# Two copies instead of one for the high part of the weights in the up projection groups without down tiles

## The reference, cut to what matters

```python
def block(xt):
    q = (xt @ wq).reshape(tb, PEER_HEADS, 2, PEER_HALF_DIM)
    ...
    gate = jax.nn.softmax(sc.astype(jnp.float32), axis=-1)
    pre = jnp.einsum("td,thkd->thk", xt, down[idx])
    act = (jax.nn.gelu(pre.astype(jnp.float32), approximate=False) * gate).astype(xt.dtype)
    return jnp.einsum("thk,thkd->td", act, up[idx])
```

## Time and profile before

| | |
|---|---|
| median of 3 runs | 2964.32 us (2959.3 to 2971.26) |
| profiled execution, its own time | 2967.73 us |
| its span | 2965.8 us |
| granted TensorE clock, mean over the span | 0.975 |
| busy: PE, PEld, DVE, ACT, POOL | 2742.1, 2529.3, 1888.9, 1127.9, 1075.9 us |

### The profile page before, as it was taken

One profiled execution on the slowest core, in us unless ns is written; L12 is line 12 of the kernel. 1 busy time (PEld: TensorE's weight loads), 2 busy tenths in 40 slices (PEclk: granted clock), 3 DMA queues, 4 the chain that ended last, 5 costly groups with the idle time before them and its releaser, 6 DMA issues.

```text
span 2965.8 us, 55557 instructions
## 1 busy us (share of the span) xinstructions
PE 2742.1 (92%) x20766; PEld 2529.3 (85%) x20766; DVE 1888.9 (64%) x3331; ACT 1127.9 (38%) x1682; POOL 1075.9 (36%) x444
## 2 busy tenths in 40 slices
PE   7899999989987999999988999999999889999997
PEld 5687777889987999999866877778999779999997
DVE  1663562299798554689817526533995975457887
ACT  1312320344487444333303124104445864443332
POOL 0000110478843656433300001004887245663332
PEclk9999999999999999999999999999999999999998
DMA  5222223255544566455452322233555446664543
GB/s 191 101 80 82 103 75 140 88 174 175 170 146 171 199 207 205 155 194 184 143 184 72 104 72 90 88 128 129 170 170 169 152 174 206 198 199 165 195 172 107
DMA packets 145453, 439.50 MB, mean 148 GB/s; under 512 B 62066, under 2 KB 63602, under 8 KB 126772
## 3 DMA queue, kind: packets, MB, share of 16 engines
q1 hardware_dynamic: 132548, 400.84, 39.7%
q10 hardware_dynamic: 12784, 37.00, 3.3%
HBM read 407.10 MB, written 30.15 MB: 147 GB/s over the span
## 4 chain that ended last, share of the span: by engine, by line
PE 61%; DVE 15%; issue 12%; POOL 8%; ACT 2%; DVEq 1%; DMA 0%; POOLq 0%; ACTq 0%; SPq 0%
PE banks L462 60%; POOL DHL L1903 7%; DVE arena L1356 3%; DVE OHE L1356 2%; DVE OHG L1356 2%; DVE ACTS L1356 1%; DVE AHL L1356 1%; ACT arena L983 1%; DVE UHL L1356 1%; POOL arena L1891 1%; DVE hT L1364 1%; DVE arena L1685 0%; DVE arena L1457 0%; DVEq L1356 0%; ACT L983 0%
## 5 line engine op out<-in xcount | busy, mean ns | idle before, releaser
L462 PE MATMUL banks<-HHL,DHL 128*128 128x264 f32 x6816 | 859.4, 287 | 23.6 <-POOL DHL L1903 12.1
L462 PEld LDWEIGHTS banks<-HHL,DHL 128*128 128x128 f32 x6816 | 844.2, 190 | 32.3 <-POOL DHL L1903 16.5
L462 PE MATMUL banks<-AHL,UHL 128*128 128x264 f32 x6144 | 773.3, 286 | 31.6 <-DVE AHL L1356 29.1
L462 PEld LDWEIGHTS banks<-AHL,UHL 128*128 128x128 f32 x6144 | 758.6, 189 | 41.9 <-issue 41.8
L1903 POOL TENSOR_TENSOR DHL<-ring,DHL 128x1024 fp32r<-128x1024 f32 x256 | 657.3, 2572 | 277.8 <-ACT DHL L983 276.0
L1356 DVE TENSOR_TENSOR xT<-xT,banks 128x264 f32<-128x264 f32 x1040 | 402.7, 423 | 388.8 <-PE banks L462 387.9
L462 PE MATMUL banks<-hT,ring 128*128 128x272 f32 (+1 forms) x2048 | 501.8, 403 | 9.7 <-issue 7.9
L1909 POOL TENSOR_TENSOR UHL<-ring,UHL 128x1024 fp32r<-128x1024 f32 x128 | 308.7, 2412 | 538.2 <-ACT UHL L983 538.2
L462 PEld LDWEIGHTS banks<-hT,ring 128*128 128x128 f32 x2048 | 394.4, 196 | 101.7 <-issue 23.1
L983 ACT ACTIVATE UHL<-ring 128x2048 fp32r<-128x2048 f32 x128 | 245.5, 1918 | 509.8 <-PE banks L462 486.7
L983 ACT ACTIVATE arena<-banks 128x264 f32<-128x264 f32 (+6 forms) x226 | 98.7, 455 | 635.9 <-PE banks L462 587.2
(11 more groups left out here) (118 smaller groups left out, 1925.1 us busy)
## 6 DMA issues: line engine op xcount, KB each, us to landing
ring<-down SPq DMA_DIRECT2D x256, 512.0 KB, 3.7
ring<-up SPq DMA_DIRECT2D x128, 1024.0 KB, 4.9
ring<-wm SPq DMA_DIRECT2D x100, 1024.0 KB, 5.0
hT<-second_gates SPq DMA_DIRECT2D x32, 528.0 KB, 4.9
second_gates<-ring ACTq DMA_DIRECT2D x12, 768.0 KB, 3.3
second_gates<-hT ACTq DMA_DIRECT2D x10, 768.0 KB, 3.3
ACTS<-extra_acts SPq DMA_DIRECT2D x2, 2112.0 KB, 9.8
arena<-hs ACTq DMA_DIRECT2D x2, 1280.0 KB, 6.1
```

The costliest lines, as they stand in the source:

```text
L462: return pe.matmul(out, lhsT, rhs, start=start, stop=stop)
```

## The change

In groups from MIXED on, ScalarE's one copy over both tiles becomes two copies of one tile each: tile 1, the one that GpSimd reads, first, and with it the release of GpSimd; then tile 0, which releases nobody. The AHL copy follows as before, with VectorE's release. In groups below MIXED the one copy stays.

```diff
-                    f(UHL[:, b, 0].rearrange("p a m -> p (a m)"),
-                      ring[:, RAWU + 2 * b:RAWU + 2 * b + 2].rearrange("p s k m -> p (s k m)"), ACT.Copy)\
-                        .then_inc(S["uhi_done"], 1)
+                    if g < MIXED:
+                        f(UHL[:, b, 0].rearrange("p a m -> p (a m)"),
+                          ring[:, RAWU + 2 * b:RAWU + 2 * b + 2].rearrange("p s k m -> p (s k m)"), ACT.Copy)\
+                            .then_inc(S["uhi_done"], 1)
+                    else:
+                        f(UHL[:, b, 0, 1], ring[:, RAWU + 2 * b + 1].rearrange("p k m -> p (k m)"), ACT.Copy)\
+                            .then_inc(S["uhi_done"], 1)
+                        f(UHL[:, b, 0, 0], ring[:, RAWU + 2 * b].rearrange("p k m -> p (k m)"), ACT.Copy)
                     f(AHL[:, b, 0], ACTS[:, bass.ds(turn * GRP + half_g * GRP, GRP), :], ACT.Copy)\
                         .then_inc(S["ahi_done"], 1)
```

## The result

The changed kernel is faster: 2941.35 us median (2935.73 to 2943.41, 6 runs) against 2965.52 us (2959.30 to 2971.26, 6 runs) for the kernel before. The ratio is 0.9903, with a 95% interval of 0.9889 to 0.9918. The profiled execution took 2936.94 us with a span of 2935.0, 30.8 us less span than before.

The account below looks back on a forecast made before the run. TensorE, busy 92% of the span, was taken as the bound, held back 33.2 us in groups 24 to 63; less 5.4 us remaining, the gain is 28 us, from 2964.3 to 2936 us, range 2928 to 2944, top set at 2950.

Parts of the forecast that it names:

- The bound and who is late: Groups 24 to 63: TensorE, pace 5.86 us a group, is held back 33.2 us by GpSimd's late start slowing VectorE.
- x = 0.87: Splitting ScalarE's UHL copy lets GpSimd start and end 0.87 us earlier, judged from ScalarE's DHL copies in the trace.
- What VectorE gets: VectorE's UHL low instruction, with GpSimd's cover shrunk to 0.33 us, takes 1.41 us.
- The margin of 0.13 us: In groups starting on time, the next could begin after 5.73 us, 0.13 before TensorE is ready at 5.86.
- the 0.14: VectorE's UHL low takes 1.22 us plus the time covered by GpSimd minus 0.14, a line through three covered cases.
- A pair gives back x up to 0.735: Two successive groups lose 0.735 us together; GpSimd starting x earlier wins back x, at most that 0.735.
- What is late next: Remainder over TensorE's pace: 0.63 us in group 25 plus 2.1 from late starts, 5.4 us in both layers, between 1.3 and 9.
- The late starts: ScalarE starts late three times in layer 0 on late loads, 0.7 us each; layer 1 taken alike.
- Rival 3: The late AHL copy holds up VectorE's low part and makes the kernel slower, 3000 us in its worst case; chance 0.03.
- a slip beyond the room: A later AHL copy, slip y, costs nothing up to about 0.75 us, then all of it; gain used up at 1.44.
- its last case: Both half copies take as long as the whole one, y = 1.9: 0.46 us per interval, 36 us over 78, 3000 us.
- TensorE's clock: A gapless TensorE might run slower; granted clock 1.00 (2.4 GHz) in the busy stretch ahead, so nothing was taken for it.

Follow-up runs that it names:

- a short GpSimd instruction: Kernel before, one copy kept, GpSimd making only 128 of its 1024 low-part columns in groups 24 to 63: 2935.07 us, 0.9881.
- -0.09 us (4 us lost): The change's two copies in the other order, tile 0 first, GpSimd's release on the second: 2971.82 us, 1.0013 of the kernel before.
- 0.43 (14.9 won): The change with the cut moved: first copy 1536 columns and GpSimd's release, second 512: 2955.69 us, 0.9961 of the kernel before.
- Room and order: The change plus eight banks of room in group 25 and SyncE's other loads moved behind the group's weights: 2931.16 us, 0.9867; again 2934.40, 0.9888.
- the kernel with room: The change, with group 25 given room for eight banks so TensorE needn't wait there for VectorE's sums: 2939.99 us, 0.9902 of the kernel before.
- y = 1.49: The change with tile 0's high part made in 16 copies of 64 columns, so the AHL copy comes late: 2961.11 us, 0.9979.
- the kernels with 8 and 22 copies: The change with tile 0's high part made in 8 copies (2942.23 us, 0.9904) or 22 copies (2988.39 us, 1.0048).

## Why the prediction was right, point by point

The forecast was 2936 us with a gain of 28; measured were 2941.35 and 24.2 by the medians, 28.8 by the ratio, and 29.1 in the stretches. The mechanism is the one forecast.

- **The bound and who is late.** Right, and shown: with a short GpSimd instruction VectorE's takes 1.22 us and the waits go.
- **The split's x = 0.87.** 1.14 us from the copy's start to GpSimd's, for 1.13 forecast from the DHL rows; x = 0.86. The two copies took 2.01 us; I wrote 2.10, since I added two lengths without their overlap. The AHL copy moved back by 0.1 us.
- **What VectorE gets.** 1.41 us forecast, 1.41 and 1.43 measured. The margin of 0.13 us was enough in every group whose data were in time. By the rule of the Trainium skill that the prediction cites, without the 0.14, it would have been 1.55.
- **A pair gives back x up to 0.735.** Shown at three shifts: -0.09 us (4 us lost), 0.43 (14.9 won) and 0.86 (29.1 won). All that could be won in the stretches was 508.6 - 474.8 = 33.8 us, 0.6 more than the prediction's 33.2, which ends at the start of group 63; late data and group 25 keep 4.7 of it.
- **What is late next.** I took 5.4 us; 4.7 were there (479.5 - 474.8). Group 25 began 6.48 us after group 24, 0.62 over the pace for 0.63 forecast. The late starts cost 2.1 us in layer 0, as I had it, and 1.4 in layer 1. There are three of them in layer 0, as forecast, but not of 0.7 us each: 9 groups from 1231.23 on took 0.47 us over the pace and the next 11, with the two others, 1.40; that the sum of three equal guesses came out is in part luck. The first, in the trace of the changed kernel:

```profile
1279.07 2.01 ACT L983 ACTIVATE UHL<-ring 128x1024 fp32r<-128x1024 f32 x2 [3.96 <-PE banks L462]
...
1281.65 2.04 DVE L1361 TENSOR_TENSOR UHL<-ring,UHL 128x1024 fp32r<-128x1024 f32 x1
...
1284.44 7.82 PE L462 MATMUL banks<-AHL,UHL 128*128 128x264 f32 x62 [0.29 <-DVE AHL L1361]
```

  VectorE's instruction takes 2.04 us there. Room and order are what this depended on: with both changed, nothing is left. What each gives was not measured apart beyond group 25's 0.6 us a layer.
- **Rival 3's price was wrong.** I charged a slip beyond the room to every group. It is charged to a pair, by the alternation that I had used two parts earlier for GpSimd and failed to apply here. Measured were 0.24 us a group for y - 1.08 = 0.41, and 0.50 for 0.96 in the pairs without an incident. The change would turn into a loss at about y = 1.08 + 0.735 = 1.8 us and not at 1.44, and for the y = 1.9 of its last case, which no run has, my estimate is now 39 x 0.82 = 32 us over the change, about the time of before and not 3000; the runs have y = 1.49 still faster than before (0.9979) and 2.04 slower (1.0048).
- **TensorE's clock** was granted at 1.00, its 2.4 GHz level, over the window from 2680 to 2918 us, as taken.

Still open: why a load of the same size and place lands sooner in one run than in another. Layer 0 took 240.1 and 240.0 us in the two traces of the change, and 245.0 in that of the kernel with room, whose loads are in the same order; the load that started it is shown in the last section, and what delayed it is not known.

## What to carry to other kernels

When one engine's instruction has two lengths by turns, look for what runs beside it, plot its length against the overlap, and ask who could start earlier. Where one instruction feeds two readers, cut it, make the part for the reader that gets in another's way first, and release that reader then; the cut alone is a small loss. And where a wait is measured against the end of the group before, a delay in one group is paid back in the next, so charge it to pairs.

## What the runs showed of the hardware

**GpSimd and VectorE block each other both ways.** The cluster of waits in the kernel with room for eight banks has both orders side by side:

```profile
1328.63 2.01 ACT L983 ACTIVATE UHL<-ring 128x1024 fp32r<-128x1024 f32 x2 [5.40 <-PE banks L462]
...
1333.19 0.70 DVE L1361 TENSOR_TENSOR AHL<-ACTS,AHL 128x528 fp32r<-128x528 f32 x1
1333.52 2.62 POOL L1914 TENSOR_TENSOR UHL<-ring,UHL 128x1024 fp32r<-128x1024 f32 x1 [1.33 <-ACT UHL L983]
1333.81 2.90 DVE L1361 TENSOR_TENSOR ACTS<-ACTS,hT 128x528 f32 x1
...
1336.79 0.38 SPq L422 DMA_DIRECT2D hT<-second_gates  x1
1337.26 4.50 SPq L403 DMA_DIRECT2D ring<-up  x2
...
1343.75 2.01 ACT L983 ACTIVATE UHL<-ring 128x1024 fp32r<-128x1024 f32 x2 [8.82 <-DMA ring<-up]
```

GpSimd's instruction starts at 1333.52, while VectorE's AHL low is running (1333.19 to 1333.89, its usual 0.70 us), and takes 2.62 us in place of 2.40. VectorE's next instruction, the product with the second gates, starts at 1333.81 under GpSimd. It takes 0.69 or 0.70 us alone (at 1325.86 and 1341.10 in this kernel), and here 2.90: it ends 0.57 us after GpSimd (1336.14 and 1336.71). So the one that came first runs as if alone, and the other stands until it ends; all but 0.13 us of the later one's own length comes behind. The same product took 2.90 and 2.89 us under GpSimd in the kernels with 8 and 22 copies (1354.45 and 2827.28). The 0.13 is the 0.14 of the prediction's line. I read it as an instruction's opening part, which goes on under the block; the rows show its size and not which part it is. The sums into xT, with one input in PSUM, took 0.43 us under GpSimd or not. This agrees with the Trainium skill (SBUF — State Buffer, "Who interferes with whom") but for that 0.13 us, which it leaves out.

**The block makes a late load later.** The same rows show how one late start becomes a cluster. ScalarE starts at 1328.63, 7.35 us after SyncE began to issue the two loads there (1321.28), where the changed kernel's trace has 5.64 at that place (1326.37 to 1332.01). The profile puts this wait down to TensorE, but at its pace ScalarE would have started about 5.86 us behind its last start of 1320.69. It was a late load, and the traces' view of the DMA issues shows it: this one landed 7.2 us after its issue, at about 1328.5, and the one of the changed kernel 5.5 us after its own. ScalarE's next copies then follow at once (1332.39), GpSimd with them, and VectorE's product falls under it. SyncE waits for that product before it loads second gates (1336.79) and only then the next group's weights (1337.26), which land 6.3 us later, and ScalarE starts on those at 1343.75. In the changed kernel's trace the products at this place took their 0.69 or 0.70 us. With the second gates behind the weights TensorE waited for nobody from group 25 on in four stretches.

**A stand of TensorE was paid for twice.** In the kernel with 22 copies such a cluster in layer 1 left TensorE standing for 5.89 us, and then its granted clock was down. This was seen once. Its timeline:

```profile
2846.75 13.87 PE L462 MATMUL banks<-AHL,UHL 128*128 128x264 f32 x96 [5.89 <-DVE AHL L1364]
```

The windows of the same kernel behind that; behind each stretch's length stand the busy times of PE, PEld, DVE, ACT and POOL, with counts in brackets, then clock, DMA share and GB/s:

```profile
2846.00:2850.00 4.00, 3.25 (x15) 3.25 (x16) 3.15 (x8) 0.97 (x5) 0.06 (x1) 0.50 0.48 182
2850.00:2854.00 4.00, 4.00 (x30) 4.00 (x30) 2.76 (x6) 0.00 (x0) 0.00 (x0) 0.87 0.19 80
2854.00:2862.00 8.00, 7.22 (x59) 7.01 (x58) 6.16 (x14) 5.75 (x28) 2.52 (x2) 1.00 0.37 131
```

0.50 is the 1.2 GHz level; 1.00 was granted again in the window from 2854 on. The packet of 96 matmuls took 13.87 us, where one at the 2.4 GHz level takes 11.96: 1.91 us beside the 5.89.
